# Handing on ring places by last use, and gathering unscaled rows, in a two-block transformer kernel

## The reference

```python
def hier_moe(h, ...):                                     # h = x * rsqrt(mean(x*x) + eps) * norm2_g
    glog = xt @ w_rg + b_rg; gsel = argmax(glog)          # 1 of 4 groups for each token
    elog = xt @ w_re + b_re                               # 4 experts in each group
    ...                                                   # top 2 experts inside the chosen group
    wts = ggate * top_p / sum(top_p)
    act = silu(einsum("nd,edf->nef", xt, w1)) * einsum("nd,edf->nef", xt, w3)
    act = act * comb[:, :, None]                          # the weight of each expert, 0 for most
    y = einsum("nef,efd->nd", act, w2)                    # x + y, then a last rmsnorm
```

## Time and profile before

| | |
|---|---|
| median of three timed runs | 810.04 us (809.05 to 810.35) |
| the profiled execution | 810.37 us, span 808.4 us |
| PE busy | 791.3 us, 98% |
| DVE, ACT, POOL busy | 58%, 54%, 56% |
| mean granted clock of PE | 0.99 |
| chain that ended last | PE 92%, DVE 5%, ACT 1%, DMA 1%, issue 1% |

### The profile page before, as it was taken

The page is one execution under the profiler, slowest core; times in us unless marked ns, Lnnn a source line. Parts: engine busy times, 40 slices in busy tenths (PEclk is TensorE's granted clock), DMA queues, the critical chain, the costliest instruction groups (busy, mean ns, idle before and its releaser), DMA issues.

```text
span 808.4 us, 15735 instructions
## 1 busy us (share of the span) xinstructions
PE 791.3 (98%) x6066; PEld 708.3 (88%) x6066; DVE 468.7 (58%) x949; ACT 437.2 (54%) x686; POOL 450.0 (56%) x351
## 2 busy tenths in 40 slices
PE   9999999999999999999999999999999899999996
PEld 7999889999999998889999999999988688788784
DVE  5853454672412225585497935437647986795864
ACT  5434654745545456785549543235447765674753
POOL 4997486999999997777975424345832000000002
PEclk9999999999999999999999999999998989999999
DMA  7765145455564554435653313133548796695801
GB/s 296 269 209 209 58 151 183 160 206 208 208 208 163 201 208 165 155 150 183 200 210 106 106 54 106 54 106 106 181 171 347 276 368 257 240 403 221 321 12 52
DMA packets 22810, 151.29 MB, mean 187 GB/s; under 512 B 2656, under 2 KB 3168, under 8 KB 5344
## 3 DMA queue, kind: packets, MB, share of 16 engines
q1 hardware_dynamic: 21312, 147.26, 50.0%
q10 hardware_dynamic: 1440, 3.21, 1.4%
HBM read 147.97 MB, written 1.05 MB: 184 GB/s over the span
## 4 chain that ended last, share of the span: by engine, by line
PE 92%; DVE 5%; ACT 1%; DMA 1%; issue 1%; DVEq 0%; SPq 0%; ACTq 0%
PE bank L1309 77%; PE bank L1880 3%; DVE w_lo L3097 1%; DMA raw<-weights_dram 1%; PE bank L1462 1%; DVE w_more_lo L3097 1%; PE bank L1476 1%; PE bank L1412 1%; PE bank L1909 0%; PE bank L2141 0%; PE bank L2096 0%; PE bank L1968 0%; PE bank L1890 0%; PE bank L2181 0%; PE bank L1485 0%
## 5 line engine op out<-in xcount | busy, mean ns | idle before, releaser
L677 POOL TENSOR_TENSOR w_lo<-raw,w_hi 128x512 fp32r<-128x512 f32 x340 | 440.2, 1331 | 151.3 <-ACT w_hi L729 140.9
L1309 PE MATMUL bank<-h_hi,w_hi 128*128 128x256 f32 x800 | 227.5, 284 | 0.2 <-DVE w_lo L2343 0.2
L1309 PE MATMUL bank<-h_hi,w_lo 128*128 128x256 f32 x800 | 222.5, 278 | 0.0
L1309 PE MATMUL bank<-h_lo,w_hi 128*128 128x256 f32 x788 | 218.6, 277 | 0.0
L729 ACT ACTIVATE w_hi<-raw 128x1024 fp32r<-128x1024 f32 x170 | 173.5, 1059 | 66.9 <-PE bank L1309 32.8
L1309 PEld LDWEIGHTS bank<-h_hi,w_hi 128*128 128x128 f32 x800 | 150.5, 188 | 4.6 <-issue 1.7
L1309 PEld LDWEIGHTS bank<-h_hi,w_lo 128*128 128x128 f32 x800 | 150.5, 188 | 0.0
L1309 PEld LDWEIGHTS bank<-h_lo,w_hi 128*128 128x128 f32 x788 | 148.3, 188 | 0.3
L1309 PE MATMUL bank<-w_hi,g 128*128 128x512 f32 x376 | 121.2, 392 | 3.4 <-DVE g L3180 1.8
L708 POOL TENSOR_TENSOR tok<-x_sb,work 128x512 f32<-128x512 f32 x2 | 2.5, 1284 | 187.9 <-DVE x_sb L3223 187.9
L1309 PEld LDWEIGHTS bank<-w_hi,g 128*128 128x128 f32 x376 | 70.6, 188 | 19.0 <-issue 2.5
(11 more groups left out here) (449 smaller groups left out, 1374.4 us busy)
## 6 DMA issues: line engine op xcount, KB each, us to landing
raw<-weights_dram SPq DMA_DIRECT2D x109, 1024.0 KB, 4.8
work<-weights_dram SPq DMA_DIRECT2D x27, 1024.0 KB, 6.6
x_sb<-x_dram SPq DMA_DIRECT2D x2, 512.0 KB, 4.4
raw<-weights_dram SPq DMA_DIRECT2D x2, 512.0 KB, 7.5
work<-final_norm_dram ACTq DMA_DIRECT2D x2, 512.0 KB, 4.0
work<-work ACTq DMA_DIRECT2D x8, 128.0 KB, 5.5
out_dram<-tok SPq DMA_DIRECT2D x3, 256.0 KB, 2.2
work<-constants_dram SPq DMA_DIRECT2D x1, 640.0 KB, 6.8
```

The costliest lines, as they stand in the source:

```text
L677: return nc.gpsimd.tensor_tensor(w_lo[:, part], raw[:, part], w_hi[:, part].bitcast(F32), ALU.subtract)
L1309: ins = mm(dst, a, b, start=start and n == 0, stop=stop and n == 2, skip_group_check=True)
```

## The change

1. Ring places are handed on in the order of release (RELEASES, sorted by last use): quarter j takes the place of the quarter that is entry j - 10 of that list (heir_of, place_of). SPLIT_AT comes from split_steps: every split stands at least one step behind the one before. Quarters 10 to 17 now stand at steps 12 to 19, one each; 44 to 47 at 48 to 51, 48 and 49 at 52 and 53; 74 and 75 at 84 and 85, 76 to 79 at 86 to 89. The places of quarters 0 to 37 stay.
2. Rows are gathered unscaled. tok_hi is made from x3 in four halves (row_hi_part) at four points in ACT's program, tok_lo by POOL in four pieces, one behind each. The copy scaled by the root is gone. The root enters as the scale of the silu (for gathered tiles a 17th column of slot_weight) and in the slot weights, which are multiplied by it before they are gathered (`scaled`, in the place of `wide`).
3. keep_warm after the router has 3 matmuls and not 6.

```diff
@@ -114,14 +114,33 @@
-def split_before(j):
-
-    if j < W_RING:
-        return max(first_use(j) - 4, FREE_STEP * (j >= W_RING - 2))
-    return max(split_before(j - 1), last_use(j - W_RING) + 2)
-
-
-SPLIT_AT = [max(split_before(j), 0) for j in range(len(STREAM))]
+RELEASES = sorted(range(len(STREAM)), key=last_use)
+
+
+def heir_of(j):
+
+    return RELEASES[j - W_RING]
+
+
+def place_of(j):
+
+    return j if j < W_RING else place_of(heir_of(j))
+
+
+def split_steps():
+
+    steps = []
+    for j in range(len(STREAM)):
+        if j < W_RING:
+            steps.append(max(first_use(j) - 4, FREE_STEP * (j >= 8), 0))
+        else:
+            assert heir_of(j) < j
+            steps.append(max(steps[-1] + 1, last_use(heir_of(j)) + 2))
+        assert j < 4 or steps[-1] + 2 <= first_use(j)
+    return steps
+
+
+SPLIT_AT = split_steps()
@@ -518,7 +537,7 @@
-            r = j % W_RING
+            r = place_of(j)
             if r == W_RING - 1:
@@ -542,7 +561,7 @@
                                    ("slot", NT), ("rank_of", NT * 4), ("place", NT * 4), ("is_rank", 16), ("ranked", NT * 16),
-                                   ("wide", NT * 4), ("weight", TILES * 16))
+                                   ("scaled", NT * 17), ("weight", TILES * 17))
         assert at_size <= 200
@@ -554,7 +573,7 @@
         rank_group = routed("rank_group").bitcast(I32)
-        rank_of, place, ranked, wide = (routed(n).rearrange("p (t n) -> p t n", t=NT) for n in ("rank_of", "place", "ranked", "wide"))
+        rank_of, place, ranked, scaled = (routed(n).rearrange("p (t n) -> p t n", t=NT) for n in ("rank_of", "place", "ranked", "scaled"))
         is_rank = routed("is_rank").rearrange("p (r g) -> p r g", r=GROUPS)
@@ -694,16 +713,16 @@
                 lo(n, n)
-            for t in range(NT):
-                for c in range(2):
+            for c in range(2):
+                for t in range(NT):
                     of = slice(c * 512, (c + 1) * 512)
-                    pool.wait_ge(sem("tok_hi_done"), t + 1)
-                    ins = nc.gpsimd.tensor_tensor(tok_lo[t][:, of], tok3[:, t, of], tok_hi[t][:, of].bitcast(F32), ALU.subtract)
-                ins.then_inc(sem("tok_lo_done"), 1)
+                    pool.wait_ge(sem("tok_hi_done"), NT * c + t + 1)
+                    nc.gpsimd.tensor_tensor(tok_lo[t][:, of], x3[:, t, of], tok_hi[t][:, of].bitcast(F32), ALU.subtract)\
+                        .then_inc(sem("tok_lo_done"), 1)
             for c in range(2):
...
                 pool.wait_ge(sem("expert_constants"), 32)
-                pool.wait_ge(sem("tok_lo_done"), NT)
+                pool.wait_ge(sem("tok_lo_done"), 2 * NT)
                 pool.wait_ge(sem("x_summed"), c + 5)
@@ -748,7 +767,7 @@
                 hi_, of = slot_ring(j)[0], slot_quarter(j)
-                act_e.wait_ge(sem("quarter_done"), N_QUARTERS + (last_use(j - W_RING) + 1 if j >= W_RING else 0))
+                act_e.wait_ge(sem("quarter_done"), N_QUARTERS + (last_use(heir_of(j)) + 1 if j >= W_RING else 0))
                 h = j // 2 - 1
@@ -1176,6 +1195,11 @@
+            def row_hi_part(t, c):
+
+                part = slice(c * 512, (c + 1) * 512)
+                nc.scalar.activation(tok_hi[t][:, part], x3[:, t, part], ACT.Copy).then_inc(sem("tok_hi_done"), 1)
+
             def tile_hi(t, k, b, j):
@@ -1184,11 +1208,14 @@
                 part_square(t, 0, stat[:, 8 + t:9 + t])
+            for t in range(NT):
+                row_hi_part(t, 0)
             prepare_root()
...
                 tile_hi(0, k, 6, k - 4)
+            row_hi_part(0, 1)
             act_e.wait_ge(sem("pair_free0"), 42)
@@ -1196,12 +1223,7 @@
             nc.scalar.activation(stat[:, 2:4], last_sums, ACT.Sqrt).then_inc(sem("last_rooted"), 1)
-            act_e.wait_ge(sem("last_summed"), 2)
-            for t in range(NT):
-                nc.scalar.activation(tok3[:, t, :], x3[:, t, :], ACT.Copy, scale=stat[:, 4 + t:5 + t])\
-                    .then_inc(sem("rows_scaled"), 1)
-                act_e.wait_ge(sem("rows_scaled"), t + 1)
-                nc.scalar.activation(tok_hi[t], tok3[:, t, :], ACT.Copy).then_inc(sem("tok_hi_done"), 1)
+            row_hi_part(1, 1)
             slot_hi_first()
@@ -1225,8 +1247,11 @@
                     act_e.wait_ge(sem("slot_product"), 1)
-                nc.scalar.activation(slot_silu, bank[n % 2][:, 0:S], ACT.Silu,
-                                     scale=stat[:, 4 + t:5 + t] if slot_tile(n) is None else 1.0).then_inc(sem("slot_silu"), 1)
+                scale = stat[:, 4 + t:5 + t]
+                if slot_tile(n) is not None:
+                    act_e.wait_ge(sem("slot_weights_ready"), 1)
+                    scale = slot_weight[:, slot_tile(n), 16:17]
+                nc.scalar.activation(slot_silu, bank[n % 2][:, 0:S], ACT.Silu, scale=scale).then_inc(sem("slot_silu"), 1)
@@ -2072,7 +2097,7 @@
             router(range(4, KD), (1,), lambda k: 8 + (k - 4) // 2 * 2 + 2).then_inc(sem("logits_ready"), 1)
-            keep_warm(1, 6, warm)
+            keep_warm(1, 3, warm)
@@ -2103,8 +2128,8 @@
                     for t in range(NT):
-                        ins = mm(bank[6][:, 16 * tile:16 * (tile + 1)], one_hot[:, t, tile * P:(tile + 1) * P].bitcast(F32),
-                                 ranked[:, t, :], start=t == 0, stop=t == 1)
+                        ins = mm(bank[6][:, 17 * tile:17 * (tile + 1)], one_hot[:, t, tile * P:(tile + 1) * P].bitcast(F32),
+                                 scaled[:, t, :], start=t == 0, stop=t == 1)
                 ins.then_inc(sem("counted"), 1)
@@ -2184,8 +2209,9 @@
                     pe.wait_ge(sem("one_hot_ready"), NT)
+                    pe.wait_ge(sem("tok_hi_done"), 2 * NT)
                     gather(tok_hi, True, False)
-                    pe.wait_ge(sem("tok_lo_done"), NT)
+                    pe.wait_ge(sem("tok_lo_done"), 2 * NT)
                     gather(tok_lo, False, True)
@@ -3144,13 +3170,12 @@
             link(ins)
-            V.tensor_reduce(routed("ranked"), by_group.rearrange("p t r i g -> p (t r i) g"), AX_X, ALU.add)\
-                .then_inc(sem("ranked_ready"), 1)
+            link(V.tensor_reduce(routed("ranked"), by_group.rearrange("p t r i g -> p (t r i) g"), AX_X, ALU.add))
+            for t in range(NT):
+                V.tensor_scalar(scaled[:, t, 0:16], ranked[:, t, :], stat[:, 4 + t:5 + t], None, ALU.mult)
+            V.tensor_copy(scaled[:, :, 16], stat[:, 4:6]).then_inc(sem("ranked_ready"), 1)
             slot_low(3)
             dve.wait_ge(sem("ranked_ready"), 1)
-            for t in range(NT):
-                ins = V.tensor_scalar(wide[:, t, :], ranked[:, t, 0:GROUP_EXPERTS], stat[:, 4 + t:5 + t], None, ALU.mult)
-            link(ins)
@@ -3166,7 +3191,7 @@
                 if tile is None:
-                    weight = wide[:, t, i:i + 1]
+                    weight = scaled[:, t, i:i + 1]
                 else:
@@ -3192,7 +3217,7 @@
                 dve.wait_ge(sem("counted"), 3)
-                V.tensor_copy(routed("weight"), bank[6][:, 0:16 * TILES]).then_inc(sem("slot_weights_ready"), 1)
+                V.tensor_copy(routed("weight"), bank[6][:, 0:17 * TILES]).then_inc(sem("slot_weights_ready"), 1)
```

## The result

The kernel after takes 799.01 us (798.74 to 799.24, four runs), the kernel before 809.54 beside it (808.75 to 810.35): ratio 0.987, interval 0.9853 to 0.9887. In a second comparison it took 800.0 (799.17 to 800.1) beside 809.13, 0.9888 (0.9872 to 0.9905). So it gains 9 to 10.5 us; forecast were 9.9 and 800.2, with a range of 799.0 to 802.4, at the lower end of which the first of the two lies. The profiled executions are 810.37 before and 799.24 after, 11.13 us apart, and it is these two whose rows are set side by side here.

A forecast was written before the change was run, and what follows sets the result against it. TensorE was taken to bound the kernel, busy 98% of the span, so only its idle or half-clock time could be won. Terms -6.1 - 3.5 - 0.3 = -9.9 us gave 800.2 us, range 799.0 to 802.4.

The forecast's parts named there:

- gap 1: Turn of unit 2: PE idles, then runs at half clock, as the product waits behind subtractions; removal saves 6.10 us.
- Gaps 2 and 3: Steps 56 and 92: PE waits for low halves behind six subtractions in a row; removal saves 3.49 us together.
- The front: Before the first expert matmul: moving POOL's subtractions makes DVE 1.9 us earlier, of which 0.3 us reaches the path.
- What is late next: PE's own filler: Before the first expert matmul: eleven keep-warm matmuls let only 0.35 us, less a hand-over, of DVE's 1.9 count.
- the forecast proper: Whole kernel: the prediction's own outcome without rivals, 799.3 to 800.9 us, chance 0.61.
- A: Front: the clock comes back late after the shorter filler, up to +1.6 us, 801.0 to 801.8; chance 0.12.
- B: Front: POOL's first two moved pieces hold up DVE's sum of squares, half a microsecond, 800.7 us; chance 0.15.
- B's milder form: Front: only POOL's first piece runs ahead of L3018; slack swallows all but 0.1 us.
- C: Steps 56 and 92: idle stays, wholly or partly, because ACT's split waits for the place's release; 803.6 us; chance 0.07.
- E: Unit 2: the product is late by something other than the subtractions, time stays 810 us; chance 0.02.
- D: Step 4 of each unit: two subtractions delay the low half, 0.6 us at 18 units, 811.0; decides above pitch 1.26; chance 0.03.

The follow-up runs named there:

- the ring alone: The kernel before with only the new ring places and split steps, its front unchanged: 800.2 us beside 809.12, ratio 0.9896.
- the run alone: The kernel after with the ring places and split steps of before, so only the front is changed: 808.23 us beside 809.12, ratio 0.9992.
- the run with POOL late: The kernel after with six fillers instead of eleven behind the counts and POOL's four subtractions held until the group is chosen: 801.62 us, ratio 0.9909.

## Why the prediction was right, and where not

**The gaps.** Right in place, cause and cure. DVE's queue behaved as walked: product at 640.3 to 640.8 with 1.2 us to spare, the low half at 643.2, no idle time of PE above 0.2 us in the experts, clock at full. The first term of the sum was mis-sized: gap 1 at 6.10. In the profile I read it from it was worth 6.1, but 2.7 of these were half clock, and that part differs by execution: the same gap was worth 5.0 in two other profiles. The median of the ring alone, 8.9 less, agrees with 5.0. I should have taken the idle part (3.4) as fixed and given the clock's part a range.

**Gaps 2 and 3** were worth 1.9 each and not 1.75: the first matmul behind a stop is followed later too, by 0.30 and 0.34 us instead of 0.23, and I counted one pitch only. The rows that follow those at 706.64 and 759.17 in the earlier trace rows (timeline of PE, kernel before):

```profile
706.94 0.39 PE L1309 MATMUL bank<-w_lo,g 128*128 128x512 f32 x1
...
759.51 0.40 PE L1309 MATMUL bank<-w_lo,g 128*128 128x512 f32 x1
```

The reason that I gave for their going, that the handed-on places move work into DVE's idle time, is not wrong for this kernel but isn't needed: one split a step is enough, on the old places.

**The front**, -0.3, was too small if anything: 0.53 by the two profiles, 0.6 or 0.9 by the run alone, with an interval that holds 0.3 too. Two steps in it are wrong. "What is late next: PE's own filler" holds where the clock is low; where it is full, the fillers end over 2 us before DVE. And in the low case an instruction behind a filler follows at its pitch and not at the end that the row shows, so that more than the 0.35 us of idle time could be won.

**Luck.** Against the ring alone the gaps were priced 0.7 us too high (gap 1 by 1.1, gaps 2 and 3 by 0.3 too low), and the front 0.2 to 0.6 too low. The two errors nearly cancel: that 800.2 lies near 799.0 to 800.0 is partly luck, and so is it that 799.01 still lies in a range that begins at 799.0: it is below the 799.3 at which the forecast proper ended, and the lower end left no room for a front worth more than 0.3.

**Rivals.** A (clock late after the shorter filler) isn't seen: with six fillers behind the router the kernel has the same time. B's milder form came true: one piece ahead of L3018, hidden; the Trainium skill's rule ("SBUF — State Buffer", "Who interferes with whom") agrees with the 1.62 against 0.69. C and E are excluded by the waits. D is excluded at this pitch, and its price was too high even past it: 0.6 us at each of 18 units against 0.1 to 0.7 at six.

## What to carry to other kernels

Where an engine works a queue in program order, look at what stands ahead of the instruction that PE waits for and when each of those pieces is itself needed; spreading early work one piece a step removes the wait without removing any work. Work for later costs when a run of it stands just ahead of a turn. An engine that is loaded beyond what the bottleneck gives it loses its lead first and then the deficit at each unit, until something (here an operand that two units share) gives it its time back; look for such losses in the distance between turns, since small ones leave no idle time in the rows. Don't size a stall from one profile when the clock falls in it, and don't call a filler the bound before seeing it at both clocks.

## What the runs showed of the hardware

An integer TENSOR_SCALAR of 128 x 4 with a single SBUF operand (L3106 of the run with POOL late) was held up by POOL for 1.00 us, where it takes 0.17 in the runs with POOL's pieces moved; in the run of the ring alone the same instruction (L3098 there) took 0.61, up to the end of POOL's first piece. I had looked only at instructions with two SBUF operands. The Trainium skill ("SBUF — State Buffer", "Who interferes with whom") says that tensor_scalar can enter a mode that uses both port pairs and can then contend with GpSimd; the rows agree that it contends, though none shows the mode.

Of two adjacent instructions with two SBUF operands, at times both were held and at times only the first (L3125 and L3126 of the ring alone, 0.94 and 0.16, though POOL was at work until 610.80 there).

The granted clock in the front fell and rose at different places in executions of the same code. The idle stretches of 1.6 us at units 8 and 14 of the kernel before, with full work around them, didn't lower it (1.00 from 704 to 712 and from 757 to 765). And not all scatter is the clock's in the front: in the four profiles with the old front the router's first matmul, which stands ahead of all changed code, started anywhere from 598.5 to 600.7.
